# Two edits of one schedule: a wait priced into the placing of steps, and the choice of experts dealt out from seven columns ahead

## What is computed

```python
def fn(t):                                    # PEER, a block of tokens
    q = (t @ wq).reshape(blk, PEER_HEADS, PEER_DKEY)
    s1 = jnp.einsum('thd,hnd->thn', q[..., :half], subkeys[:, 0])
    s2 = jnp.einsum('thd,hnd->thn', q[..., half:], subkeys[:, 1])
    v1, i1 = lax.top_k(s1, PEER_TOPK)
    v2, i2 = lax.top_k(s2, PEER_TOPK)
    cand = (v1[..., :, None] + v2[..., None, :]).reshape(blk, PEER_HEADS, PEER_TOPK * PEER_TOPK)
    sc, pos = lax.top_k(cand, PEER_TOPK)
    e = (jnp.take_along_axis(i1, pos // PEER_TOPK, axis=-1) * N_KEYS
         + jnp.take_along_axis(i2, pos % PEER_TOPK, axis=-1))
    g = jax.nn.softmax(sc, axis=-1)
    a = jax.nn.gelu(jnp.einsum('td,thkd->thk', t, u[e]))
    return jnp.einsum('thk,thkd->td', g * a, v[e])
```

## Time and profile before

| | |
|---|---|
| time, median of 3 runs | 1810.5 us (1807.15 to 1812.6) |
| the profiled execution's own time | 1809.06 us |
| its span, first to last instruction | 1807.2 us |
| PE, DVE, ACT, POOL busy in the span | 69%, 72%, 32%, 29% |
| DMA | 696.47 MB, 385 GB/s over the span |
| gathers (queue 0) | 570.53 MB of it |
| mean granted clock of PE | 0.771 |

### The profile page before, as it was taken

The page is one execution under the profiler, slowest core; times in us unless marked ns, Lnnn a source line. Parts: engine busy times, 40 slices in busy tenths (PEclk is TensorE's granted clock), DMA queues, the critical chain, the costliest instruction groups (busy, mean ns, idle before and its releaser), DMA issues.

```text
span 1807.2 us, 26391 instructions
## 1 busy us (share of the span) xinstructions
PE 1254.0 (69%) x9056; PEld 696.8 (39%) x9056; DVE 1310.1 (72%) x3857; ACT 579.8 (32%) x1995; POOL 527.0 (29%) x569
## 2 busy tenths in 40 slices
PE   8989877678877575788876576679877544434343
PEld 3677532445545232454534233446545111111111
DVE  5563796889666667898766668999666768686754
ACT  2231133333423333333333234343333222222222
POOL 0100232233322322333322323333322433333332
PEclk9989888688898596877899597887998555555555
DMA  6237799999999999999999999999999999999997
GB/s 266 78 95 292 282 414 422 363 425 424 402 423 423 424 423 418 375 396 403 425 423 421 425 422 383 425 389 401 420 423 420 414 427 426 425 427 426 426 416 305
DMA packets 119380, 696.47 MB, mean 385 GB/s; under 512 B 17983, under 2 KB 21118, under 8 KB 49102
## 3 DMA queue, kind: packets, MB, share of 16 engines
q0 software_dynamic: 78848, 570.53, 75.8%
q1 hardware_dynamic: 36686, 121.83, 17.4%
q10 hardware_dynamic: 3712, 2.43, 0.4%
HBM read 691.65 MB, written 3.02 MB: 384 GB/s over the span
## 4 chain that ended last, share of the span: by engine, by line
DMA 31%; DVE 28%; PE 25%; issue 7%; ACT 4%; POOL 1%; ACTq 1%; DVEq 0%; POOLq 0%
DMA rows<-in_peer_uv,index 22%; DVE rows L2646 11%; PE ps_v L1814 6%; PE ps_f L1553 4%; DMA wch<-in_w_row 3%; PE ps_f L1568 3%; DMA wch<-in_w_out 3%; PE ps_h L1794 2%; PE ps_f L1347 2%; DVE score L2322 2%; DMA wch<-in_w_uq 1%; DVE best L2321 1%; PE ps_f L1431 1%; PE ps_f L1471 1%; ACT diag L2158 1%
## 5 line engine op out<-in xcount | busy, mean ns | idle before, releaser
L1324 POOL DMA_INDIRECT rows<-in_peer_uv,index x544 | 517.2, 951 | 1183.1 <-PE ps_v L1814 1004.3
L2646 DVE CUSTOM_DVE_ANT_0 rows<-rows,ps_h 128x1024 f32<-128x1024 f32 x544 | 656.4, 1220 | 269.7 <-DMA rows<-in_peer_uv,index 203.3
L1814 PE MATMUL ps_v<-rows,diag 128*32 128x256 f32 x4352 | 425.1, 507 | 428.0 <-ACT diag L2158 414.7
L1814 PEld LDWEIGHTS ps_v<-rows,diag 128*32 128x32 f32 x4352 | 125.5, 131 | 680.6 <-ACT diag L2158 549.8
L2149 ACT ACTIVATE tan<-arg 128x2 f32<-128x2 f32 x272 | 55.4, 204 | 782.9 <-DVE arg L2656 704.7
L2152 ACT ACTIVATE weight<-tan,lead 128x1 f32<-128x1 f32 x544 | 180.8, 379 | 9.2
L2158 ACT ACTIVATE diag<-sel,weight 128x32 f32<-128x32 f32 x544 | 140.9, 306 | 0.4 <-PE ps_v L1814 0.3
L1553 PEld LDWEIGHTS ps_f<-bufh,wch 128*128 128x128 f32 x768 | 113.6, 232 | 21.2 <-issue 19.0
L1553 PE MATMUL ps_f<-bufh,wch 128*128 128x128 f32 x768 | 119.6, 320 | 0.0
L1347 PE MATMUL ps_f<-wch,bufh 128*128 128x512 f32 (+1 forms) x192 | 84.6, 583 | 22.9 <-DMA wch<-in_w_row 20.7
L1347 PEld LDWEIGHTS ps_f<-wch,bufh 128*128 128x128 f32 x192 | 34.2, 209 | 68.5 <-issue 37.6
(11 more groups left out here) (398 smaller groups left out, 1685.5 us busy)
## 6 DMA issues: line engine op xcount, KB each, us to landing
wch<-in_w_gate SPq DMA_DIRECT2D x60, 512.0 KB
wch<-in_w_row SPq DMA_DIRECT2D x36, 512.0 KB
wch<-in_w_o SPq DMA_DIRECT2D x32, 512.0 KB
wch<-in_w_out SPq DMA_DIRECT2D x24, 512.0 KB
wch<-in_peer_wq SPq DMA_DIRECT2D x24, 512.0 KB
rows<-in_peer_uv,index POOLq DMA_INDIRECT x544
w_tok<-in_w_tok SPq DMA_DIRECT2D x4, 1640.0 KB, 13.7
wch<-in_w_uq SPq DMA_DIRECT2D x6, 384.0 KB
```

Of the source, the lines that this page charges most:

```text
L1324: pool.indirect_dma_start(rows[c % RING][:, :, :].rearrange("p a d -> p (a d)"), None, io.peer_uv[:, :], at).then_inc(s_uv[c % RING], 16)
L1814: ins = nc.tensor.matmul(ps_v[GROUP * a:GROUP * (a + 1), :], diag[:, c % DRING, :], rows[c % RING][:, 1, QD * a:QD * (a + 1)], start=False ...
L2646: v.tensor_tensor_reduce(out=u, in0=u, in1=ps_h[:, :], scale=1.0, scalar=0.0, op0=ALU.mult, op1=ALU.add, accum_out=dots[:, c % KEEP:c % KE ...
```

## The change

Two things are changed. First, `step_work` adds `HANDS` = 2.4 us to PE's cost at x = 27 (the heads' copies) and at k = 0 (the first scores). The steps and their order stay; the columns on which they stand move, since the sum of costs is laid evenly. Second, the parts of the choice of block n are placed by a table: where block n isn't the first of its tile (`BLOCKS[n][1] > 0`), at -7, -4, -1, 2, 5, 8, 11, 14, 17, 19 and 22 from the start of block n - 1. Block 1 and the first blocks of tiles (5, 9, 13) keep their columns. No instruction is added or taken away.

```diff
+HANDS = 2.4
+AHEAD = (-7, -4, -1, 2, 5, 8, 11, 14, 17, 19, 22)
...
-    pe_head = {5: DC * small, 8: 7 * small, 13: 3 * small, 16: 4 * 0.67 + 2 * wide, 23: 9 * small, 26: 2 * H * small}
+    pe_head = {5: DC * small, 8: 7 * small, 13: 3 * small, 16: 4 * 0.67 + 2 * wide, 23: 9 * small, 26: 2 * H * small, 27: HANDS}
...
+        if k == 0:
+            pe += HANDS
...
+def choice_columns():
+
+    at = {}
+    for n in range(1, NB):
+        first = SG * (n - 1)
+        for j in range(PARTS):
+            if n == 1:
+                k = CHOICE_AT + j
+            elif BLOCKS[n][1] > 0:
+                k = AHEAD[j]
+            else:
+                k = 2 * (j + 1)
+            at[first + k] = (n, j)
+    return at
+
+
+CHOICES = choice_columns()
...
-                    if n == 0 and 0 <= k - CHOICE_AT < PARTS:
-                        choose(1, k - CHOICE_AT)
-                    if 0 < n < NB - 1 and k % 2 == 0 and 1 <= k // 2 <= PARTS:
-                        choose(n + 1, k // 2 - 1)
+                    if b in CHOICES:
+                        choose(*CHOICES[b])
```

## The result

The changed kernel took 1816.45 us in the median of 20 runs, the kernel before 1810.49 in 20 runs beside them: a ratio of 1.0037, with a 95% interval from 1.0024 to 1.0050. It is slower by 6 to 7 us, where 10 us of gain were forecast; 1800.5 was 16 us off, and the range of 1790 to 1811 did not hold the result.

What follows compares the result with a forecast made beforehand. DMA at its full rate was taken to bound most of the span. Terms summed to 10.0 us returned, taking the profiled 1809.06 to 1799.1; with the median 1.4 above, the forecast was 1800.5 us, range 1790 to 1811.

Steps and rivals of the forecast that it cites:

- What bounds the kernel: Whole span: DMA's full rate sets most of the time; only slower stretches can return time, 30 us at most.
- The first edit, passes 1 and 2: First scores of passes 1 and 2: mixes and gathers come sooner, returning 4.5 of 6.3 and 2.0 of 5.8 us.
- Pass 3: ... Nothing: Start of block 9: the turning stays ahead of `spread(9)`, DVE's wait of 6.10 us stays, nothing is returned.
- The second edit, block 6: Pass 2: two parts ahead of `head_spin` delay the turning 3.3 us; behind it 2.0 us return at 780, 0.3 at 830.
- Block 10: Pass 3: two parts delay the turning and `spread(9)`, losing 3.3 us; third free; 1.5 us each return at 1180 and 1250.
- Pass 1, the table's 1.5 us at 450: Block 3's moved parts were to return 1.5 of the 2.3 us lost in the stretch at 450 to 460.
- slower: Rival: parts ahead of `head_spin` delay the turnings, blocks 7, 8, 11, 12 lose over 2 us each; 1819 us, chance 0.10.
- Given and taken: Rival: pass 1 returns 6 us, passes 2 and 3 nothing or -3; 3 to 6 us, middle 1806, chance 0.20.
- The gather near 342: Sign in pass 1: no gather after a gap of over 5 us near 342.
- The eighth slice: Sign in pass 1: this slice's DMA rate rises from 363 to above 390 GB/s.
- The seventeenth: Sign in pass 2: this slice's DMA rate rises from 375 to 390 GB/s or so.
- The twenty-fifth: Sign in pass 3: this slice's DMA rate falls below 383 GB/s, the next three slices higher in sum.

Runs made afterwards that it cites:

- e5_no_pass3: Kernel before plus HANDS in passes 1 and 2 only, choice on its old columns; 1803.07 us, ratio 0.9967 to the kernel before.
- e12_base_again: The same program as e5_no_pass3 run once more; 1805.03 us, ratio 0.9976 to the kernel before.
- e1_hands: Changed kernel with the choice back on its old columns, so HANDS alone in all passes; 1808.61 us, ratio 0.9993 to the kernel before.
- e16_hands_again: The same program as e1_hands run once more; 1810.02 us, ratio 1.0000 to the kernel before.
- the base: The program with HANDS in passes 1 and 2 only and the old choice, run as e5_no_pass3 and e12_base_again; mean ratio 0.9972.
- e9_only_pass3: Kernel before plus HANDS in pass 3 alone, choice on its old columns; 1812.29 us, ratio 1.0010 to the kernel before.
- e14_ahead_2_3_4: As e5_no_pass3, with the table of the choice for blocks 2, 3 and 4 only; 1806.29 us, ratio 0.9973 to the kernel before.
- e15_ahead_rest: As e5_no_pass3, with the table for blocks 7, 8, 14, 15 and 16 only; 1800.98 us, ratio 0.9960 to the kernel before.
- e4_only_6_10: Kernel before with the table for blocks 6 and 10 only, HANDS = 0; 1814.96 us, ratio 1.0020 to the kernel before.
- e11_in_front: As e5_no_pass3, with the table for blocks 6 and 10 only; 1808.57 us, ratio 0.9993 to the kernel before.
- e3_keep_6_10: Changed kernel with blocks 6 and 10 keeping their old columns of the choice; 1813.29 us, ratio 1.0023 to the kernel before.
- e2_ahead: Changed kernel with HANDS = 0, so the table of the choice alone; 1817.66 us, ratio 1.0040 to the kernel before.
- e10: As e5_no_pass3, with the choice of blocks 6 and 10 begun early but behind head_spin; 1802.55 us, ratio 0.9965 to the kernel before.
- e18_late_again: As e5_no_pass3, plus HANDS's columns in pass 3 for steps behind the turning (x above 26), repeating an earlier run; 1805.41 us, ratio 0.9976.

## Why the prediction was wrong, by its own steps

**What bounds the kernel**, DMA wherever its rate is full: right. Losses and gains behind the first dot stood in the stretches below 424 GB/s, and after column 383 the rates did not change. The 4.2 us ahead of the first dot were in no term.

**The first edit, passes 1 and 2: right in kind.** Forecast 4.5 + 2.0 us; e5_no_pass3 and e12_base_again, which have nothing else, gave 0.28% in the mean, 5.2 us. From first dot to first dot pass 1 took 391.1 to 395.8 us in every profile with HANDS or the table in it, 396.2 to 398.3 in the three without. DVE's wait of 5.06 us is gone there (at the first `index_unit` of the kernel after it is 0.54 us, and none at the second). In pass 2 the waits of 10.2 us were 2.43 and 2.72 us in e12_base_again, about the 4 forecast.

**"Pass 3: ... Nothing": the step that failed for the first edit.** It measured 4.5 us of loss (e1_hands and e16_hands_again against the base; 1.8, within noise, in e9_only_pass3). From first dot to first dot pass 3 took 403.5 and 406.0 us in the first two and 398.0 and 398.4 in the base's two; it took 399.0 in e9_only_pass3 and 398.9 before. Single profiles scatter by as much, though: e14_ahead_2_3_4 and e15_ahead_rest, with no HANDS in pass 3, took 404.4 and 403.5 (the last section says how they differ, and e16_hands_again with them), so the 4.5 us rest on the ratios of 12 runs each. I had looked only at the turning and the first scores, which hardly move in relation to each other, and took the rest of the pass for unchanged. But a cost in a running sum doesn't open a gap at one place. It pulls the steps ahead of it together and pushes all behind it back: in pass 3 x = 16 to 24 stand one column sooner, up to two after k = 4, and one until about k = 60. No row of mine asked what waits at those steps. That this shift costs is what the runs show; which of the moved steps does it is open.

**The second edit, block 6: the mechanism right, the term mis-sized and set against the wrong partner.** I priced it at 3.3 us and hid it in the 2.0 us for the first edit, as if the turning alone mattered. All three parts delay the first `index_unit`: the distance grew by 6.0 us in e4_only_6_10, by 5.7 in e11_in_front and by 4.0 between e3_keep_6_10 (727.88 - 690.08 = 37.8) and the changed kernel (41.8). DVE's waits for the ReLU don't take them up, since these waits follow the turning: in e4_only_6_10, which has them, the first grew from 5.51 to 6.29 us. What I hoped for behind it did come: 2.9 and 1.9 us at 780 and 830, where 2.0 and 0.3 were forecast, though e1_hands, without the table, has the first of them as well (426 GB/s). It was less than the 5.3 lost ahead of it and the 1.4 each at 630 and 860.

**Block 10: mechanism and price right, its surroundings not.** Two top 16 put the first dot of block 9 off by 3.5 us in e4_only_6_10; 3.3 were forecast. The third went under DVE's wait, as forecast: 6.10 us became 4.62. In DMA rate the loss was 5.0; PE's granted clock in the stretch was 0.67 where it had been 0.90, but no run separates what that cost. In the changed kernel 1.2 and 1.0 us came back later of the 3.0 forecast. With the second edit alone more did: 2.1 and 2.8 us in e4_only_6_10, and 2.3 and 2.7 in e2_ahead (407 and 418 GB/s). So the return too was rightly seen for this edit by itself; beside HANDS in pass 3 most of it failed to come. It isn't certain either: e11_in_front had 1.9 us back at 1180 against e12_base_again and 3.3 less at 1250.

**Pass 1, the table's 1.5 us at 450: the dip closed, the time did not change.** With the table in all blocks the stretch moved 425 GB/s in the changed kernel, 426 in e2_ahead and 430 in e3_keep_6_10; with HANDS and no table in pass 1 it was 397, 423, 392, 370 and 342 (e1, e5, e10, e11, e12). But e14_ahead_2_3_4 stands at 0.9973 beside its base's 0.9972.

**The rivals.** The one called slower named this mechanism, two parts ahead of `head_spin`, 3.3 us in each pass, and asked for losses over 2 us in blocks 7, 8, 11 and 12. No such loss came: in the changed kernel columns 0 to 11 of blocks 7, 8, 11 and 12 (905 to 940, 1007 to 1041, 1311 to 1346 and 1414 to 1441 us) moved 423, 424, 422 and 425 GB/s, and the dip at 860 stands at column 211, in the middle of block 6. The time came out slow with less than it asked for: the losses ahead of the turning, an unlooked-for loss in pass 3 from the first edit, and a late start. I held 27.10 of 28 us of DVE busy in my hand as evidence for it, and gave it one chance in ten. "Given and taken", at 0.20, had the balance of the passes right, pass 1 up and the other two not, and the losses too small.

**The signs.** The gather near 342 no longer came after a gap of over 5 us (4.75 and 3.37). The eighth slice reached 387, short of the 390 named. The seventeenth stayed at 376, against the 390 named, which was block 6's loss; the eighteenth was above 410, at 425. The twenty-fifth fell as named, but the three behind it came to 1206 in sum, where 1215 had stood and more was named. No low stretch opened at the start of blocks 7, 8, 11 or 12.

In percent, the ledger: -0.28 (HANDS, passes 1 and 2), +0.25 (HANDS, pass 3; 0.10 by the other comparison), +0.20 (blocks 6 and 10), and 0 to +0.25 for the rest of the table, together +0.02 to +0.42. Measured: +0.37. At the middle of the first three it is +0.17, so about half of what was measured rests on the table's unexplained rest, which the late start of 4.0 us, 0.22%, would fill if it were so in every run.

## What to carry to other kernels

Work may be moved forward only into an engine's idle time, and the stretch to look at is the one up to the next thing that somebody else waits for: 27.10 busy of 28 us ahead of a hand-over to PE meant here that 5.1 us of added work became 6.0 us of delay. The same parts a few columns later, behind that hand-over, cost no time that could be measured, though they delayed the same places by 2.4 us.

When a planner lays a sum of costs evenly, one more cost moves steps all over the pass, some of them forward. List all columns that change, in each pass, and ask at every one what it now waits for. Price a wait in the passes where it exists: two of three gained, and the third gave most of it back.

With effects of 0.1 to 0.3% add single results only if they were repeated. Two repeats here held up (e12_base_again, e16_hands_again), one did not by its ratio (e18_late_again).

## What was unexpected of the hardware

The same four matmuls of `spread(9)`, with the same columns for all of pass 3's steps, ran at two speeds. In e14_ahead_2_3_4:

```profile
L1819 PE MATMUL ps_h<-hrows,rep x4: 1056/1056/1217, 1115.1 to 1117.8; 32*128 32x512 f32 x4
...
  DVE rows L2671: 8.0, 1
```

In e12_base_again:

```profile
L1819 PE MATMUL ps_h<-hrows,rep x4: 587/587/692, 1108.2 to 1109.6; 32*128 32x512 f32 x4
...
  DVE rows L2671: 5.6, 1
```

The first row gives the shortest, median and longest in ns, 1056 against 587; the second is how long DVE waited for them, 8.0 against 5.6 us. The stretches around it, e14_ahead_2_3_4 first and then e12_base_again:

```profile
1105.00:1110.00 5.00, 0.05 (x4) 0.00 (x0) 4.86 (x13) 0.61 (x3) 1.90 (x2) 0.50 1.03 421
1110.00:1115.00 5.00, 4.48 (x24) 3.28 (x24) 0.85 (x5) 2.42 (x6) 0.94 (x1) 0.50 0.99 383
1115.00:1120.00 5.00, 5.00 (x14) 1.54 (x14) 1.08 (x1) 1.77 (x6) 0.00 (x0) 0.50 0.42 179
1120.00:1125.00 5.00, 5.00 (x23) 2.63 (x24) 4.79 (x19) 0.98 (x2) 2.36 (x3) 0.50 0.66 213
```

```profile
1095.00:1105.00 10.00, 3.32 (x27) 1.02 (x26) 9.37 (x27) 3.70 (x13) 2.54 (x3) 0.50 1.02 418
1105.00:1110.00 5.00, 5.00 (x24) 3.37 (x20) 0.00 (x0) 3.23 (x9) 0.94 (x1) 0.75 0.96 360
1110.00:1115.00 5.00, 5.00 (x43) 3.03 (x43) 4.65 (x13) 1.18 (x3) 2.81 (x3) 1.00 0.60 193
```

Both come to the turning (1111.53 in the first, 1105.26 in the second) at a granted clock of 0.50 of 2.4 GHz, which is 1.2 GHz, after PE had had little to do. In the second the clock rose to 2.4 GHz during the turning; in the first PE was busy without a break from then on and stayed at 1.2 GHz until about 1130, through the spread and the first mixes and scores. From `query_sums` to the first dot of block 9 it was 1118.92 - 1086.57 = 32.4 us in e14_ahead_2_3_4 and 30.0 in e12_base_again, and the stretch 1100 to 1150 moved 345 GB/s against 387, 5.0 us, though both have the same steps and choice there. Three of the twenty profiles had it so (e14, e15 and e16, with waits of 8.01, 8.01 and 8.00 us); in the others the wait was 6.5 us or less. It makes a single profile of this stretch uncertain by 2 to 5 us. Whether it is a source of the scatter between runs of one kernel, 8 to 17 us over 12 runs, isn't shown, as only one run of each was traced. The Trainium skill (TensorE: Matmul & The Clock Gate, What's actually happening) says that activity releases a throttled clock; the trace agrees, but how soon it was released differed here between two kernels with the same work at this place.
